# Recurrent unit's input factor applied to projected blocks, and unread products in two waits for layer norm factors

## The reference

```python
def layer_norm(x, g, b):
    mu = xf.mean(-1, keepdims=True)
    var = jnp.mean(jnp.square(xf - mu), -1, keepdims=True)
    return ((xf - mu) * lax.rsqrt(var + LN_EPS)).astype(x.dtype) * g + b

def rms_norm(x, g):
    y = xf * lax.rsqrt(jnp.mean(xf * xf, axis=-1, keepdims=True) + RMS_EPS)
    return (y * g.astype(jnp.float32)).astype(x.dtype)

def rglru_mixer(h, w_in, conv_w, conv_b, w_a, b_a, w_x, b_x, lam, w_out):
    u = h @ w_in
    xb, gate = u[..., :D_RNN], u[..., D_RNN:]
    xb = causal_depthwise_conv(xb, conv_w, conv_b)
    r = sigmoid(blockdiagonal(xb, w_a) + b_a)
    i = sigmoid(blockdiagonal(xb, w_x) + b_x)
    log_a = -C_RG * r * softplus(-lam)
    bt = sqrt(-expm1(2.0 * log_a)) * (i * xb)
    hseq = linear_recurrence(exp(log_a), bt)
    y = hseq * silu(gate)
    return y @ w_out
...
        h = rms_norm(x, norm_pre[layer])
        o = rglru_mixer(h, ...)
        x = x + rms_norm(o, norm_post[layer])
```

## Time and profile before

| | us |
| --- | --- |
| median of 3 runs | 1841.34 |
| lowest, highest | 1837.76, 1843.67 |
| the profiled execution | 1838.0 |
| its span | 1836.2 |
| TensorE busy | 1740.1 (95%) |
| VectorE busy | 1132.7 (62%) |
| ScalarE busy | 822.5 (45%) |
| GpSimd busy | 713.0 (39%) |
| mean granted TensorE clock | 0.986 |

### The profile page before, as it was taken

How to read it: one execution, slowest core, us unless ns; L and a number is a source line. 1 busy time by engine, 2 the same in 40 slices (tenths; PEclk the granted TensorE clock), 3 DMA queues, 4 the chain that set the end, 5 groups by cost and what they waited for, 6 DMA issues and landing times.

```text
span 1836.2 us, 31937 instructions
## 1 busy us (share of the span) xinstructions
PE 1740.1 (95%) x12808; PEld 1376.6 (75%) x12808; DVE 1132.7 (62%) x1515; ACT 822.5 (45%) x1233; POOL 713.0 (39%) x488
## 2 busy tenths in 40 slices
PE   7999999988998999999989997999989999999996
PEld 7777777778776777777787874665767888887875
DVE  6676687775566118878774744668728264636454
ACT  3433655453635344645543624367634333323342
POOL 2554543420343435633320441433444434334342
...
GB/s 361 267 256 77 91 92 87 104 32 4 195 92 66 171 80 81 92 87 104 76 27 85 138 101 95 141 56 65 82 147 128 91 68 82 67 72 81 69 92 104
DMA packets 63188, 193.01 MB, mean 105 GB/s; under 512 B 5936, under 2 KB 6192, under 8 KB 62672
## 3 DMA queue, kind: packets, MB, share of 16 engines
...
HBM read 173.25 MB, written 17.83 MB: 104 GB/s over the span
## 4 chain that ended last, share of the span: by engine, by line
PE 56%; issue 23%; POOL 9%; DVE 7%; ACT 4%; POOLq 0%; ACTq 0%; DVEq 0%
PE proj L2429 37%; POOL w_lo_sb L709 9%; PE aux L2448 4%; PE aux L2696 2%; DVE area_sb L1422 2%; PE aux L2609 1%; PE aux L2459 1%; DVE slots_sb L1425 1%; PE aux L3141 1%; PE aux L3147 1%; PE aux L2470 1%; PE aux L3138 1%; DVE slots_sb L1422 1%; DVE slots_sb L2119 1%; PE proj L2696 1%
## 5 line engine op out<-in xcount | busy, mean ns | idle before, releaser
L709 POOL TENSOR_TENSOR w_lo_sb<-w_raw_sb,w_hi_sb 128x512 fp32r<-128x512 f32 x462 | 688.4, 1512 | 1000.1 <-ACT w_hi_sb L800 999.9
L2429 PE MATMUL proj<-act_hi_sb,w_hi_sb 128*128 128x512 f32 x1480 | 601.0, 406 | 10.8 <-ACT stage_sb L1216 2.6
L2429 PE MATMUL proj<-act_hi_sb,w_lo_sb 128*128 128x512 f32 x1480 | 578.1, 391 | 0.0
L2429 PE MATMUL proj<-act_lo_sb,w_hi_sb 128*128 128x512 f32 x1480 | 577.1, 390 | 0.0
L800 ACT ACTIVATE w_hi_sb<-w_raw_sb 128x1024 fp32r<-128x1024 f32 x231 | 244.3, 1057 | 659.7 <-PE proj L2429 467.0
L2429 PEld LDWEIGHTS proj<-act_hi_sb,w_hi_sb 128*128 128x128 f32 x1480 | 278.1, 188 | 93.8 <-issue 27.8
L2429 PEld LDWEIGHTS proj<-act_lo_sb,w_hi_sb 128*128 128x128 f32 x1480 | 278.6, 188 | 61.8 <-issue 7.7
L2429 PEld LDWEIGHTS proj<-act_hi_sb,w_lo_sb 128*128 128x128 f32 x1480 | 278.2, 188 | 59.8
L2448 PE MATMUL aux<-act_hi_sb,w_hi_sb 128*128 128x512 f32 x336 | 137.9, 410 | 23.6 <-issue 18.2
L1422 DVE TENSOR_TENSOR area_sb<-area_sb 128x256 f32<-128x256 f32 (+1 forms) x180 | 117.9, 698 | 45.1 <-PE aux L2610 27.5
L2448 PE MATMUL aux<-act_lo_sb,w_hi_sb 128*128 128x512 f32 x336 | 133.9, 398 | 0.0
...
## 6 DMA issues: line engine op xcount, KB each, us to landing
w_raw_sb<-wall SPq DMA_DIRECT2D x231, 512.0 KB, 3.3
area_sb<-w_ada SPq DMA_DIRECT2D x32, 512.0 KB, 5.3
...
```

The costliest lines, as they stand in the source:

```text
L709: nc.gpsimd.tensor_tensor(w_lo[:, b % 2, :, :].rearrange("p k n -> p (k n)")[:, half], w_raw[:, b % 2, half], w_hi[:, b % 2, :, :].rearran ...
L2429: ins = MM(bank, w[:, s, k, :], a[:, t, :], start=(start and i == 0), stop=(stop and i == len(terms) - 1))
```

## The change

Four things are done.

1. `keep_busy`: seven products of the ones matrix with `scan64` into a bank that the next group overwrites, behind the variance of layer norm 0, and five behind that of layer norm 1. Nobody reads them.
2. Behind layer norm 1 VectorE makes the projection's input from the scaled tile with combined columns (`pre_scale`, `pre_shift`: gain and bias of the layer norm times the gain of the root mean square norm), without the factor. ScalarE squares the tiles into `SQ`, VectorE adds the squares up, and TensorE sums them in two products (four passes) ahead of the eighth tile, instead of sixteen passes before the first. Gain and bias for x itself follow behind all splits.
3. The factor `RS` is multiplied into the projected blocks: VectorE reads all of them from PSUM, the first four into slots 8 to 11 of `G_S`, x blocks into `wa` or `spare`, g blocks into `G_S`. ScalarE's copies of x blocks are gone; its sigmoid reads `G_S`. The product with the sigmoid is a step of its own, `lru_gate`.
4. VectorE's list in the recurrent unit is written in another order. The convolution starts at a shifted column in place of reading three zeros ahead of the tile.

The diff, cut:

```diff
@@ ScalarE
-            for m in range(KT):
-                act.wait_ge(S("x_done"), KT + m + 1)
-                square("pre0", m, xa[:, m, :])
-            inverse_root(RS, "rms_pre0", 1.0 / D, 1e-6, S("rms_rs"))
...
             for m in range(KT):
+                act.wait_ge(S("ln_scaled"), KT + m + 1)
+                A(SQ[:, m, :], xa[:, m, :], ACT.Square, scale=V("ln_g1", m), bias=V("ln_b1", m)).then_inc(sq_ready, 1)
                 high(SPLITS["lru_h"] + m, m, ST[m % 2])
                 if m > 2 and m % 2:
                     weights(LRU + m // 2 + 1)
+            inverse_root(RS, "rms_pre0", 1.0 / D, 1e-6, S("rms_rs"))
             weights(LRU + 5)
-            for i in range(4):
-                x = group_ready(act, ("lru_in", 0, i))
-                act.wait_ge(S("conv_done"), i + 1)
-                job_read(A(ST[(LRU + i) % 2], x, ACT.Copy), ("lru_in", 0, i))
...
-                if half == "x":
-                    read(A(ST[b % 2], x, ACT.Copy), b)
-                else:
-                    A(ST[b % 2], x, ACT.Sigmoid).then_inc(S("sig_staged"), 1)
+                if half == "g":
+                    evacuated(act, b)
+                    if j > 1:
+                        act.wait_ge(S("lru_gated"), j - 1)
+                    A(ST[j % 2], G_S[:, j, :], ACT.Sigmoid).then_inc(S("sig_staged"), 1)
@@ VectorE, behind layer norm 1
-                    for m in range(KT + 1):
+                    def lru_h(m):
+                        if m > 1:
+                            dve.wait_ge(split_lo, n + m - 1)
+                        dve.wait_ge(S("ln_scaled"), KT + m + 1)
+                        TS(ST[m % 2], xa[:, m, :], DV["pre_scale"][:, m:m + 1], DV["pre_shift"][:, m:m + 1],
+                           ALU.mult, ALU.add).then_inc(split_src, 1)
+
+                    for m in range(KT + 2):
                         if m < KT:
                             tt(xa[:, m, :], xa[:, m, :], merged[:, 0, :], ALU.mult).then_inc(S("ln_scaled"), 1)
-                        if m:
-                            dve.wait_ge(S("ln_scaled"), KT * l + m)
-                            TS(xa[:, m - 1, :], xa[:, m - 1, :], V(f"ln_g{l}", m - 1), V(f"ln_b{l}", m - 1),
-                               ALU.mult, ALU.add).then_inc(S("x_done"), 1)
+                        if 0 < m <= KT:
+                            lru_h(m - 1)
+                        if m > 1:
+                            low(n + m - 2, m - 2, ST[m % 2])
+                        if 2 < m < KT + 1:
+                            add_squares("pre0", (m - 2,))
+                    dve.wait_ge(sq_ready, SQUARES["pre0"] + 8)
+                    for m in range(KT):
+                        TS(xa[:, m, :], xa[:, m, :], V("ln_g1", m), V("ln_b1", m), ALU.mult, ALU.add)\
+                            .then_inc(S("x_done"), 1)
...
+            def lru_scaled(j):
+                b = lru_piece("x", j)
+                read(tt((spare, wa)[j % 2][:, :], projected(dve, b), RS, ALU.mult), b)
+                evacuated(dve, b)
...
+            def lru_g(j):
+                b = lru_piece("g", j)
+                read(tt(G_S[:, j, :], projected(dve, b), RS, ALU.mult), b)
+
+            def lru_gate(j):
+                dve.wait_ge(S("sig_staged"), 8 + j + 1)
+                evacuated(dve, lru_piece("g", j))
+                tt(G_S[:, j, :], G_S[:, j, :], ST[j % 2], ALU.mult).then_inc(S("lru_gated"), 1)
+
+            dve.wait_ge(S("rms_rs"), 1)
             for j in range(4):
+                x = group_ready(dve, ("lru_in", 0, j))
+                job_read(tt(G_S[:, 8 + j, :], x, RS, ALU.mult), ("lru_in", 0, j))
...
             lru_inputs(3)
-            lru_block("g", 9)
-            for o in range(3):
+            lru_g(9)
+            lru_square(3, 0)
+            lru_gate(9)
+            for o in range(1, 3):
                 lru_square(3, o)
-            lru_block("g", 10)
+            lru_g(10)
             lru_scan(3, 0)
-            lru_block("g", 11)
+            lru_gate(10)
+            lru_g(11)
             low_y(4)
+            lru_gate(11)
             lru_scan(3, 1)
@@ TensorE
+                def keep_busy(job, n):
+                    x = job_open(pe, job)
+                    for _ in range(n):
+                        MM(x, C("ones"), C("scan64"), start=True, stop=True)
...
                     job_full(MM(var, C("ones"), ln_sq[:, 7, :], start=False, stop=True), ("ln_var", l))
+                    keep_busy(("rw", 1, 3), 7)
...
                     sum_squares(("ln", l), ("ln_var", l))
+                    keep_busy(("lru_in", 0, 3), 5)
...
-            sum_squares("pre0", "rms_pre0")
-            side_by_side(("lru_in", 0), range(KT), fresh=SPLITS["lru_h"])
+            def pre0_sum(k):
+                if k == KT - 1:
+                    added_squares(1, "rms_pre0", SQUARES["pre0"] + 8)
+
+            side_by_side(("lru_in", 0), range(KT), fresh=SPLITS["lru_h"], ready=pre0_sum)
```

153 lines of the change are left out of this document (76 added, 77 removed).

## The result

| | before | changed |
| --- | --- | --- |
| median, us (7 runs each) | 1839.95 | 1851.33 |
| lowest, highest | 1837.76, 1843.67 | 1845.61, 1854.03 |
| the profiled execution, its span | 1838.0, 1836.2 | 1846.77, 1845.0 |

The changed kernel takes 1.0053 times as long (95% interval 1.0038 to 1.0067), that is 9.8 us more (7.0 to 12.3). The ratio is formed over all runs; the two medians alone lie 11.4 us apart. The forecast was 1849.5 us, slower by 8.2.

A forecast was written before the change was run, and what follows sets the result against it. TensorE, busy 95% of the span, was taken as the bound. 8.7 us lost at the unit's end minus 0.5 saved in layer norm 0 gave +8.2: 1846.2 profiled, 1849.5 with the runs' 3.3 offset; range 1836 to 1855, the forecast's own 1845 to 1854.

The forecast's parts named there:

- Layer norm 0: Layer norm 0: seven unread products keep TensorE's clock full, saving 0.5 us, bounds 0 and 1.8.
- The split ahead of the factor: Layer norm 1: first product of the recurrent unit 14.3 us sooner; 14.7 us won when the eight tiles end.
- What is late next: Start of the recurrent unit: x4's load waits behind x's store; TensorE stands still 10.7 us, 4.0 of 14.7 us left.
- Twenty more instructions on VectorE: Recurrent unit: 12 us more on VectorE, mostly absorbed; holding TensorE costs 1.6 us, leaving 1.7 of 3.3.
- The end of the unit: End of the recurrent unit: VectorE's low part 6, which TensorE waits for, comes 8.7 us later, bounds 0 and 12.
- VectorE is 1.9 us late at its low parts 0 to 3: End of the unit, group 2: 4.4 us of added products and waits against 1.7 to 2.5 in hand.
- A scan that waits for root, sigmoid and g10's read in turn: End of the unit, after low parts 0 to 3: 2.6 us on VectorE, including a 1.3 us table load.
- The two-SBUF instructions: End of the unit: one of three sigmoid products meets a GpSimd instruction, 1.1 us more; the skill's rule could add 2.2.
- TensorE stays the bound: Rival, recurrent unit: VectorE's additions fall into its idle time, TensorE keeps 4.0 and 1.8 us; 1835.5 us, chance 0.18.
- Half of it: Rival, recurrent unit: VectorE holds x5, but the end absorbs the twelve products; 1839 us, chance 0.22.
- The unread products do not hold the clock: Rival, both layer norms: the clock falls anyway behind the unread products, losing only 0.5 us; 1850 us, chance 0.10.
- The two signs of being wrong: Recurrent unit: x4 starts within 3 us of the eighth tile, or TensorE's waits behind 1296 stay below 4 us.

The follow-up runs named there:

- e3: Changed kernel with SyncE's loads of x4 and g0 issued ahead of its wait for x and the store: 1843.36 us, ratio 1.0028 to the kernel before.
- e8: Changed kernel with loads of x4, g0 and g1 ahead of the store, gate matrices in four loads: 1835.18 us, ratio 0.9984 to the kernel before.
- e10: Changed kernel with e8's load order, ScalarE's weights and roots earlier, and VectorE's reads and gate products reordered: 1824.63 us, ratio 0.9932 to the kernel before.
- e4: Changed kernel with ScalarE's high parts of g11 and the output's first two blocks ahead of rates and sigmoids: 1846.18 us, ratio 1.0043 to the kernel before.
- e4 to e8: Five variants of the changed kernel: weights earlier (1.0043), also roots earlier (1.0024), sigmoid from PSUM (1.0031), one VectorE instruction per g block (0.9990), loads spread (0.9984).

## Why the prediction was right or wrong

**Direction and size: right, closer than the working earned.** 1851.33 against 1849.5, inside the range and inside the forecast's own range; +9.8 against +8.2. Two things helped. The forecast stands on a median of three runs, 1841.34, which with seven is 1839.95; on that it would have been 1848.2. And the two profiled executions differ by +8.8 only because the later one was 2.3 us ahead in code that the change leaves alone: behind the mark 8.7 was forecast and 10.9 measured.

**Layer norm 0: right.** Full clock at 565 to 570, and 0.4 us where 0.5 was put, since VectorE's fifth split sets the pace. One reading under it was off: the 2.33 us before 1096.95 in the earlier trace rows are those of the weight loads, while TensorE's products paused for 1.54 us only, as the view of TensorE shows:

```profile
1096.98 7.67 PE L2470 MATMUL aux<-stage_sb,const_sb 128*128 128x512 f32 x16 [1.54 <-ACT stage_sb L815]
```

The clock held over the longer 1.93 us behind layer norm 1 all the same.

**The split ahead of the factor: right** in the first product (-14.4 against -14.3). The eighth tile was 1.2 us later than forecast: VectorE's two-SBUF instructions met GpSimd's there (1.78 us for a low part at 1121.24), and TensorE waited 0.5 us for it.

**What is late next: right in kind.** The load behind x, store and all, holds x4, by 10.6 us from store to high part where 9.5 was taken from the earlier trace rows; x4 came 3.0 us sooner in place of 4.0. e3 and e8 show that it was this load: without it 12.7 us come back. Its cost is thus somewhat greater than the wait's own 10.25 us: the half clock behind the wait (x4 to g0, 1.2 GHz until about 1149.5) comes on top. The figure of the Trainium skill, "DMA: Bandwidth & Descriptors", section "Where 436 GB/s comes from", would have had x4 start 3.3 us sooner than it did (7.3 us, an estimate, against 10.6 from the store to the high part); the row was nearer. Over 1131 to 1150 the DMA engines moved 374 GB/s, more than that figure, so the rate was not what made x4 late: other transfers shared it.

**Twenty more instructions on VectorE: failed in part.** "1.7 us are left of 3.3 at the last gate product". What was left of it was less than nothing: +0.6. The waits were as foreseen in kind, 1.4 us before x8, but the step left out the clock: it is at half behind the wait before x5, now 2.98 us long, where it had stayed full behind the 0.98 us of the earlier trace rows; that costs 1.6 us. No half clock followed where that wait was absent or short (x5 to group 0 took 16.4 us in e3 and 16.5 in e10).

**The end of the unit: right in size, in part by luck, and wrong in where the time is lost.** The sum 8.7 measured 10.8. From group 3 on it had 10.4 (8.7 and the 1.7 in hand) and 10.2 were measured. The term mis-sized was "VectorE is 1.9 us late at its low parts 0 to 3": low part 1 is 3.65 us late (194.82 behind the mark, before 191.17), while low part 0 is not late at all (190.54, before 190.57). The step before, which left +0.6 and not -1.7, explains that by itself. All behind it is 7.1 us against 6.8. "A scan that waits for root, sigmoid and g10's read in turn" is the row at 1309.73. What the step did not see is that ScalarE's queue also holds the high parts of the weights, one behind the rates of group 3 (at 1295.07, where ScalarE had waited 3.7 us for VectorE) and one behind that sigmoid: TensorE waited 3.2 us for each. The sum has no term for that order, yet e4, which changes nothing else, makes the stretch 3.2 us shorter: so the terms that it did have were probably too large by about as much. Also, "VectorE near 90% from 1240 on" did not come true: it was busy 62.6 of the 80 us from 1240 to 1320, 78%, less than the 66.7 before, as it stood waiting for ScalarE.

**The two-SBUF instructions: right.** In the changed kernel's trace one of the last three gate products took 1.76 us (from 1313.42, while GpSimd worked from 1311.69 to 1314.63) and two 0.68 (no GpSimd instruction beside them), as the sum had it. By the rule of the Trainium skill ("SBUF — State Buffer", section "SBUF: two separate sides") all three could have been held, 2.2 us more. The trace agrees with the rule for the one that met GpSimd; how many do is a matter of the timeline.

**The rivals.** "TensorE stays the bound" fell: VectorE did not have g0 out in time. With SyncE's order alone (e8) TensorE still waited 3.4 us before x5, and only e10, with all three orders changed, kept that wait at 0.6 us. "Half of it" fell: the end did not absorb the products. "The unread products do not hold the clock" fell: 1.00 behind both layer norms (565 to 575 and 1108 to 1114), where e1, without them, has 0.51 at 1114 to 1120. The Trainium skill ("TensorE: Matmul & The Clock Gate", section "What's actually happening") says that activity releases the throttle; these traces agree.

**The two signs of being wrong.** Neither came: x4 starts 10.4 us behind the eighth tile, and TensorE's waits behind 1296 sum to 10.0 us. But 7.2 of these are for GpSimd's low parts and only 2.8 for VectorE's, while the working had put VectorE alone there.

**Left open.** Why a wait of 3.2 us before 1297.54 left the clock full and one of 3.25 before 1313.00 brought it to half was not tried. The runs of the changed kernel scatter over 8.4 us, those of before over 5.9. The mean granted clock of an execution goes the same way: 0.986, 0.986 and 0.984 in the three of the changed kernel below 1848 us, 0.983 to 0.985 in the four above 1851. And from x5 to group 0, with the same code there, the traces of e1 and e4 to e8 took 18.8 to 19.4 us against 18.1. So half clocks probably make part of the scatter, but only one execution of each kernel was profiled.
